# Stores, pair steps and first splits moved between engines in a fused attention, delta-rule and expert layer

## The chip, the cores and the metric

The kernel runs on one core of a Trainium2 chip. The core has a matrix engine (TensorE), a vector engine (VectorE), a scalar engine (ScalarE), GpSimd, and SyncE, which computes nothing. In this kernel SyncE, ScalarE and GpSimd issue transfers, each into its own queue in the trace, and the core's 16 DMA engines serve them all. The metric is the device time of one execution in microseconds, as the median of several runs.

## The reference

One layer in float32 on 512 tokens of width 1024. First come sliding-window attention with sinks (8 heads of 64, window 128) and a gated delta rule (4 heads of 128, chunks of 64) side by side, then the output weights `w_out` and a residual. The second half is an expert layer with product keys, and it takes most of the time:

```python
q = (xt @ w_q).reshape(T, 8, 2, 64)
s = einsum('thpc,hpnc->thpn', q, sub_keys)          # 128 keys in each half
s_top, i_top = top_k(s, 16)                         # then the 16 best of the 16 x 16 sums
gate = softmax(best_s)
act = gelu(einsum('tkd,td->tk', u_tab[idx], xn))    # 128 experts a token, out of 16384
out = h + einsum('tk,tkd->td', act * gate, v_tab[idx])
```

## The kernel before

Every matrix product is made of three, of a high and a low half of each operand in the reduced type: high by high, low by high, high by low. So each operand is split first: ScalarE copies the high half, and VectorE (or GpSimd) subtracts it from the original to get the low one. The program is a row of stages, each a block in which every engine has its own ordered list of instructions: `input_projection`, `prepare_mixers` (about 157 to 261 us), `recurrence` (to 321), `output_projection` (to 408), `routing` (to 857) and `experts` (to the end). PSUM banks are handed round by `Banks`, in the order in which their uses are added.

`prepare_mixers` makes for each of four blocks of 128 tokens the products of keys with keys (`kk`) and with queries (`qkT`), and from the first a chain of five levels that inverts a triangular matrix. `level_0` makes its first matrices (L1015) from which TensorE transposes `B0T` (L810), and `start` (L1021, L1023) makes the start of the inverse, which the levels (L749) work on. `keep_turning` (L167) issues matmuls of the identity between stages.

The expert layer is dense for tokens 128 to 511, and sparse for tokens 0 to 127. For the dense part there are 128 tiles of `u` and `v`, each 128 experts by 1024. An up product is 24 matmuls of 128x384 (L1980 to L1982 in routing, L2252 to L2254 in experts), followed by a gelu on ScalarE, and a down product is 18 matmuls of 128x512 (L2264 to L2266). Routing makes 80 up products (`EARLY`): 27 first, then one for each of 48 batches of 8 tokens, then 5 more. ScalarE stores their gelus in HBM from its own queue (L2039). Each batch also makes 16 small matmuls (L2007) of one-hot matrices, which VectorE and ScalarE prepare (L2098, L2046); ScalarE evicts them to `gate_stage` (L2062), and after every second batch SyncE stores 1 MB of gates in HBM (L1947), in the same ordered list as the loads of the u tiles (L1935, L1937), which go round 4 buffers (`NU`). Experts makes the other 48 up products, each beside a down product, and then 80 down products alone.

For tokens 0 to 127 GpSimd gathers single rows of a joint table (L1795), and VectorE takes 128 dot products (L1802) and 128 weighted sums (L1819), the pair steps, about 1.2 us each. `pair_steps` deals them out over the places, which are one batch of routing or one tile of experts. It adds a rate at each place and gives out steps while one is due, in groups of four dots and four adds; an add can't stand in the place of its own group's last dot.

```python
for rate in rates:
    due += rate
    here = []
    while at < len(todo) and due >= 1.0:
        what, k = todo[at]
        if what == "add" and k % GRP4 == 0 and ("dot", k + GRP4 - 1) in here:
            break
        here.append(todo[at])
        at, due = at + 1, due - 1.0
```

The rates give 145 steps to the first 48 places of experts, with one to six in a place, and in the last two of them one dot, and then four adds and a dot.

Of the kernel before, what the change touches and what calls it, by code (L numbers as in the profile page):

```python
# [6 lines left out]

# [5 lines left out]
P = 128  # L13
T = 512
TB = T // P
D = 1024
# [650 lines left out]
def prepare_mixers(nc, m, ps, sem, sinks, att_out_g, w_att_in, w_out):  # L667
# [16 lines left out]
    for b in range(TB):  # L684
        banks.add(("kk", b), "dve")
        banks.add(("qkT", b), "dve")
        if b:
            banks.add(("B0T", b - 1), "dve")
    banks.add(("B0T", TB - 1), "dve")
# [16 lines left out]
    with ExitStack() as ctx:  # L706
# [23 lines left out]
        with nc.Block() as block:  # L730
# [12 lines left out]
            def _(pe):  # L743
# [70 lines left out]
                for b in range(TB):  # L814
                    for g in ("kk", "qkT"):
                        banks.wait_free(pe, (g, b))
                        for h in range(DN):
                            rhs = m.unitT[:, (DN + h) if g == "kk" else h, b * P:(b + 1) * P]
                            t = nc.tensor.matmul(banks.bank((g, b))[:, h * P:(h + 1) * P],
                                                 m.unitT[:, DN + h, b * P:(b + 1) * P], rhs, start=True, stop=True)  # L820
                        t.then_inc(done, 1)
                    if b:
                        level_0_turn(b - 1)
                level_0_turn(TB - 1)
# [139 lines left out]
            def _(dve):  # L964
# [62 lines left out]
                for b in range(TB):  # L1027
# [12 lines left out]
                    if b:  # L1040
                        start(b - 1)
                start(TB - 1)
# [30 lines left out]
def recurrence(nc, m, ps, sem, wa_in, w_out_in, w_q_in, w_out, w_q, dn_out_g, x):  # L1073
# [20 lines left out]
    o_sq, o_ss, o_pow = sem("o_sq"), sem("o_ss"), sem("o_pow")  # L1094
# [3 lines left out]
    with ExitStack() as ctx:  # L1098
# [18 lines left out]
        with nc.Block() as block:  # L1117
# [68 lines left out]
            def _(dve):  # L1186
# [36 lines left out]
                for c in range(NC):  # L1223
# [51 lines left out]
            def _(act):  # L1275
# [8 lines left out]
                for c in range(NC):  # L1284
# [189 lines left out]
def output_projection(nc, m, ps, sem, w_out_in, w_q_in, early_u_in, u_t, norm_ffn_g, w_q, keys, h_dram, sel):  # L1474
# [33 lines left out]
    with ExitStack() as ctx:  # L1508
        sb = m.mem.local(ctx)
        gain = sb("ffn_gain", [P, D])  # L1510
        mixs = sb("mixT_split", [P, 2, KO, T], F32R)
        mixh, mixl = mixs[:, 0], mixs[:, 1]
        wh = sb("w_oq_h", [P, 4, KO, T], F32R)
# [7 lines left out]
        with nc.Block() as block:  # L1521
            @block.sync
            def _(sp):
                sp.dma_start(gain[:], norm_ffn_g[0:1, :].broadcast_to([P, D])).then_inc(g_in, 16)
                v = w_q[0].rearrange("(k p) n -> p k n", p=P)
                for i in range(2):

                    sp.wait_ge(w_lo, i + 1)
# [11 lines left out]
            def _(pe):  # L1540
# [15 lines left out]
                def hidden(g):  # L1556
                    half, b = g[1:]
                    pe.wait_ge(w_lo, half + 1)
# [4 lines left out]
                            lambda k: wh[:, half, k, :], lambda k: wl[:, half, k, :]).then_inc(done, 1)  # L1563

                def queries(g):
                    th, j = g[1:]
                    pe.wait_ge(w_lo, 4 if j < 2 else 6)
                    banks.wait_taken(pe, ("xT", 2 * th + 1, 1))
                    banks.wait_free(pe, g)
                    for e in range(2):  # L1570
                        h = 2 * j + e
                        v, c = slice((h % 4) * P, (h % 4 + 1) * P), slice(th * TH, (th + 1) * TH)
                        at = 2 if h < 4 else 0
# [41 lines left out]
            def _(act):  # L1615
                def split_w(i):
# [7 lines left out]
                    nc.scalar.activation(wh[:, i % 4], raw[i % 4], ACT.Copy).then_inc(w_hi, 1)  # L1624
# [28 lines left out]
                split_w(0)  # L1653
# [21 lines left out]
                for j in range(4):  # L1675
                    query_out(1, j)
                scores_out(2)
# [13 lines left out]
            def _(dve):  # L1691
                def split_w(i):
                    dve.wait_ge(w_hi, i + 1)
                    nc.vector.tensor_tensor(wl[:, i % 4], raw[i % 4], wh[:, i % 4].bitcast(F32),
# [35 lines left out]
                split_w(0)  # L1730
# [101 lines left out]
def pair_steps(rates):  # L1832
# [18 lines left out]
def routing(nc, m, ps, sem, u_in, next_u, u_t, v_rows, gates, gelus, pairs_of_0, steps, sel, nxt):  # L1851
# [6 lines left out]
    u_hi, u_lo = sem("early_u_hi"), sem("early_u_lo")  # L1858
# [45 lines left out]
    with ExitStack() as ctx:  # L1904
# [22 lines left out]
        with nc.Block() as block:  # L1927
            @block.sync
            def _(sp):
# [550 lines left out]
```

## Time and profile before

| | us |
|---|---|
| median of 3 runs | 1594.64 (1594.32 to 1595.9) |
| the profiled execution | 1595.65 |
| its span in the trace | 1593.9 |
| TensorE busy | 1527.5 (96%) |
| VectorE busy | 1322.2 (83%) |
| ScalarE busy | 715.8 (45%) |
| GpSimd busy | 349.2 (22%) |

The times of rows are microseconds from the span's start. A timeline's row is start, duration, engine, line, operation, output and inputs by their names, how many such instructions in a row, and in brackets how long the engine was idle before it and what released it. PE is TensorE, DVE VectorE, ACT ScalarE, POOL GpSimd, and SPq and ACTq are SyncE's and ScalarE's issues of transfers. Stretches of one engine overlap a little at their ends.

### The profile page before, as it was taken

Reading aid. Unit: us, or ns where it says so; the run is one execution under the profiler, and the core shown is the slowest. Engines: PE = TensorE matmul, PEld = TensorE weight load, DVE = VectorE, ACT = ScalarE, POOL = GpSimd, SP = SyncE. Lnnn points to the kernel's source line nnn. Section 1 sums busy time; section 2 is a strip of 40 time slices with the busy share of each in tenths; the row PEclk is TensorE's granted clock in tenths of the full one; section 3 lists DMA queues with packets and bytes.
Section 4 is the critical chain, followed back from the end, with each engine's and each line's share of the span. In section 5 each row is a group of like instructions: output and inputs, shape, how many; then the busy total and the mean of one; then the engine's idle time right before and its main releaser. Section 6 shows DMA issues by size and latency. Waiting matters only on the chain. (4 is left out here: it accounts for less than half of the span.)

```text
span 1593.9 us, 24872 instructions
## 1 busy us (share of the span) xinstructions
PE 1527.5 (96%) x9451; PEld 1389.4 (87%) x9451; DVE 1322.2 (83%) x2328; ACT 715.8 (45%) x1410; POOL 349.2 (22%) x301
## 2 busy tenths in 40 slices
PE   7999799999999999999998999999999999999999
PEld 6898688789999999999998999999999788888887
DVE  4638777776799999898874989998989889999996
ACT  4553453151343698788763333333333334333332
POOL 4011620110466100302230323232332211111100
PEclk9999899999999999999998999999999999999999
DMA  6220004030454477878997889898998899999972
GB/s 194 86 80 1 8 29 161 28 125 35 133 172 155 155 216 218 319 226 304 343 377 279 316 326 367 335 373 325 363 341 317 352 392 385 373 345 352 363 275 97
DMA packets 149931, 384.11 MB, mean 241 GB/s; under 512 B 10816, under 2 KB 91840, under 8 KB 131136
## 3 DMA queue, kind: packets, MB, share of 16 engines
q1 hardware_dynamic: 119872, 232.75, 41.8%
q0 software_dynamic: 18432, 134.23, 21.7%
q10 hardware_dynamic: 11520, 15.73, 2.7%
q8 instruction: 65, 1.06, 0.3%
q14 instruction: 42, 0.34, 0.1%
HBM read 337.58 MB, written 45.09 MB: 240 GB/s over the span
## 5 line engine op out<-in xcount | busy, mean ns | idle before, releaser
L1795 POOL DMA_INDIRECT scores<-in_peer_uv,pair_index x86 | 131.9, 1534 | 577.5 <-DVE pair_sum L1819 448.3
L1980 PE MATMUL bank<-x_hi,u_split 128*128 128x384 f32 x640 | 220.6, 345 | 16.4 <-DVE u_split L1917 10.8
L1982 PE MATMUL bank<-x_hi,u_split 128*128 128x384 f32 x640 | 215.9, 337 | 0.0
L1981 PE MATMUL bank<-x_lo,u_split 128*128 128x384 f32 x640 | 215.8, 337 | 0.0
L2264 PE MATMUL bank<-v_hi,act_hi 128*128 128x512 f32 x528 | 207.5, 393 | 3.4 <-DVE v_lo L2327 3.4
L2266 PE MATMUL bank<-v_hi,act_lo 128*128 128x512 f32 x528 | 206.9, 392 | 0.0
L2265 PE MATMUL bank<-v_lo,act_hi 128*128 128x512 f32 x528 | 206.7, 392 | 0.0
L2301 ACT ACTIVATE act_hi<-act_tile 128x384 fp32r<-128x384 f32 x128 | 66.9, 522 | 205.5 <-PE bank L2266 135.7
L2343 DVE TENSOR_TENSOR act_tile<-gelu_tile,onehots 128x384 f32<-128x384 f32 x128 | 117.9, 921 | 48.8 <-ACT gelu_tile L2312 37.3
L1980 PEld LDWEIGHTS bank<-x_hi,u_split 128*128 128x128 f32 x640 | 121.2, 189 | 18.7 <-ACT early_gelu L2036 10.3
L2252 PE MATMUL bank<-x_hi,u_split 128*128 128x384 f32 x384 | 129.1, 336 | 1.4 <-PEq L1927 1.4
L2254 PE MATMUL bank<-x_hi,u_split 128*128 128x384 f32 x384 | 129.0, 336 | 0.0
L2253 PE MATMUL bank<-x_lo,u_split 128*128 128x384 f32 x384 | 128.9, 336 | 0.0
L1981 PEld LDWEIGHTS bank<-x_lo,u_split 128*128 128x128 f32 x640 | 121.2, 189 | 0.0
L1982 PEld LDWEIGHTS bank<-x_hi,u_split 128*128 128x128 f32 x640 | 121.0, 189 | 0.0
L2046 ACT ACTIVATE onehot_gated<-onehot_i,rt_smallT 128x128 f32<-128x128 f32 x384 | 117.2, 395 | 7.2 <-DVE onehot_i L2098 6.8
L2264 PEld LDWEIGHTS bank<-v_hi,act_hi 128*128 128x128 f32 x528 | 99.8, 189 | 23.3 <-issue 3.8
L2266 PEld LDWEIGHTS bank<-v_hi,act_lo 128*128 128x128 f32 x528 | 99.7, 189 | 21.5
L2265 PEld LDWEIGHTS bank<-v_lo,act_hi 128*128 128x128 f32 x528 | 99.9, 189 | 19.6
L1795 POOL DMA_INDIRECT pair_rows<-in_peer_uv,pair_index x42 | 62.7, 1493 | 233.3 <-DVE pair_sum L1819 227.2
L1819 DVE SCALAR_TENSOR_TENSOR pair_sum<-scores,pair_c,pair_sum 128x1024 f32<-128x1024 f32 x86 | 107.4, 1282 | 0.7
L2327 DVE TENSOR_TENSOR v_lo<-v_raw,v_hi 128x1024 fp32r<-128x1024 f32 x88 | 107.2, 1219 | 0.4 <-ACT v_hi L2295 0.4
(325 smaller groups left out, 3654.9 us busy)
## 6 DMA issues: line engine op xcount, KB each, us to landing
v_raw<-in_peer_v SPq DMA_DIRECT2D x128, 512.0 KB, 7.2
u_raw<-in_peer_u SPq DMA_DIRECT2D x64, 512.0 KB, 6.2
u_raw_more<-in_peer_u SPq DMA_DIRECT2D x64, 512.0 KB, 6.9
gates<-gate_stage SPq DMA_DIRECT2D x24, 1024.0 KB, 5.8
onehots<-gates SPq DMA_DIRECT2D x16, 1536.0 KB, 10.8
early_gelus<-early_gelu ACTq DMA_DIRECT2D x80, 192.0 KB, 3.1
gelu_tile<-early_gelus SPq DMA_DIRECT2D x80, 192.0 KB, 7.1
w_raw<-in_w_in SPq DMA_DIRECT2D x9, 1024.0 KB, 5.2
```

The costliest lines, as they stand in the source:

```text
L1795: pool.indirect_dma_start(self.slot(k), None, self.table, bass.IndirectOffsetOnAxis(ap=self.sidx[:, k:k + 1], axis=0)).then_inc(self.lande ...
L1980: nc.tensor.matmul(banks.bank(g)[:, 0:TD], uh[:, q, w], m.xh[:, k, P:], start=(k == 0), stop=False)
L1981: nc.tensor.matmul(banks.bank(g)[:, 0:TD], uh[:, q, w], m.xl[:, k, P:], start=False, stop=False)
L1982: t = nc.tensor.matmul(banks.bank(g)[:, 0:TD], ul[:, q, w], m.xh[:, k, P:], start=False, stop=(k == KD - 1))
L2046: ins = nc.scalar.activation(og[:, slot(b, k), t, :], oi[:, slot(b, k), t, :], ACT.Copy, scale=smallT[:, b % 2, 1, k * BT + t:k * BT + t + 1])
L2252: nc.tensor.matmul(bank, uh[:, q, w], m.xh[:, k, P:], start=(k == 0), stop=False)
L2253: nc.tensor.matmul(bank, uh[:, q, w], m.xl[:, k, P:], start=False, stop=False)
L2254: t = nc.tensor.matmul(bank, ul[:, q, w], m.xh[:, k, P:], start=False, stop=(k == KD - 1))
L2264: nc.tensor.matmul(bank[:], ah[:, s, w], v_hi[:, c], start=first, stop=False)
L2265: nc.tensor.matmul(bank[:], ah[:, s, w], v_lo[:, c], start=False, stop=False)
L2266: t = nc.tensor.matmul(bank[:], al[:, s, w], v_hi[:, c], start=False, stop=last)
L2343: nc.vector.tensor_tensor(af[:], ge[n % NG2][:], gt[:, it % 2, :, jj], ALU.mult).then_inc(gate_f, 1)
```

## The change

Five edits. In `prepare_mixers` a list `opening` sets a new order of the banks of `kk`, `qkT` and `B0T` on TensorE, and VectorE's order follows it. The first half of `w_out` is split in the recurrence, into a buffer of its own (`w_first`), and the remaining weights take other places of `w_oq_h`. The first two u tiles are split at the end of `output_projection` (`u_split` now lies in the place of the first weights in `w_oq_h`) and not at the start of routing; GpSimd's low halves start with tile 2. The stores of the gates are issued by ScalarE, after the eviction of every second batch, and not by SyncE. `pair_steps` gives a place at most its rate rounded up, and the rates are 3.3 for 44 places and then 2.0 and 1.0, where they were 3.1 for 46. That gives 151 steps to the first 48 places of experts, at most four in one, and in the last two of them two adds and one add.

```diff
+    opening = [("kk", 0), ("qkT", 0), ("kk", 1), ("qkT", 1), ("B0T", 0), ("kk", 2), ("qkT", 2), ("kk", 3), ("B0T", 1),
+               ("B0T", 2), ("qkT", 3), ("B0T", 3)]
+    for g in opening:
+        banks.add(g, "dve")
...
-                for b in range(TB):
+                def gram(b):
                     dve.wait_ge(strict, 3 * b + 3)
                     banks.wait_full(dve, ("kk", b))
...
+                    banks.wait_taken(dve, ("kk", b))
+                    level_0(b)
+
+                def qk(b):
                     banks.wait_full(dve, ("qkT", b))
                     nc.vector.tensor_tensor(m.qkT[:, b], h4(banks.bank(("qkT", b))[:]), decT[:, b],
                                             ALU.mult).then_inc(banks.taken["dve"], 1)
-                    banks.wait_taken(dve, ("kk", b))
-                    level_0(b)
-                    if b:
-                        start(b - 1)
-                start(TB - 1)
+                gram(0)
+                qk(0)
+                gram(1)
+                qk(1)
+                start(0)
+                gram(2)
+                qk(2)
+                gram(3)
+                start(1)
+                start(2)
+                qk(3)
+                start(3)
...
+                    if c in (4, 6):
+                        dve.wait_ge(first_hi, 1)
+                        v = slice(c - 4, c - 2)
+                        nc.vector.tensor_tensor(m.w_first[:, 1, v, :], m.w_raw[0][:, KA + c - 4:KA + c - 2, :],
+                                                m.w_first[:, 0, v, :].bitcast(F32), ALU.subtract)
...
+                    if c == 3:
+                        act.wait_ge(w_out_in[0], 16)
+                        nc.scalar.activation(m.w_first[:, 0], m.w_raw[0][:, KA:], ACT.Copy).then_inc(first_hi, 1)
...
-
-                    sp.wait_ge(w_lo, i + 1)
+                    if i:
+                        sp.wait_ge(w_lo, 1)
                     sp.dma_start(raw[i], v[:, i * KO:(i + 1) * KO, T:]).then_inc(w_q_in[1], 16)
...
-                split_w(0)
                 for b in range(TB):
                     banks.wait_full(act, ("mixT", b))
...
                 for j in range(4):
                     query_out(1, j)
+                    if j == 2:
+                        for i in range(2):
+                            act.wait_ge(early_u_in[i], 16)
+                            banks.wait_full(act, ("q", 1, 1))
+                            nc.scalar.activation(uh[:, i, :], m.u_raw[i], ACT.Copy).then_inc(nxt.u_hi, 1)
...
+                for i in range(2):
+                    dve.wait_ge(nxt.u_hi, i + 1)
+                    nc.vector.tensor_tensor(ul[:, i, :], m.u_raw[i], uh[:, i, :].bitcast(F32),
+                                            ALU.subtract).then_inc(nxt.u_lo, 1)
                 scores_out(2)
                 scores_out(3)
...
-        while at < len(todo) and due >= 1.0:
+        while at < len(todo) and due >= 1.0 and len(here) < math.ceil(rate):
...
-                    if (k + 1) * BT % ST == 0:
-                        q = ((k + 1) * BT // ST - 1) % 2
-                        banks.wait_taken(sp, ("G", b, k, BT // 4 - 1))
-                        t0 = (b - 1) * P + (k + 1) * BT - ST
-                        sp.dma_start(gates[:, :, t0:t0 + ST, :].rearrange("g i t j -> i g (t j)"),
-                                     stage[:, q].rearrange("p g t j -> p g (t j)")).then_inc(stored[q], 16)
...
+                    if (k + 1) * BT % ST == 0:
+                        banks.wait_taken(act, ("G", b, k, BT // 4 - 1))
+                        t0 = (b - 1) * P + (k + 1) * BT - ST
+                        act.dma_start(gates[:, :, t0:t0 + ST, :].rearrange("g i t j -> i g (t j)"),
+                                      stage[:, half].rearrange("p g t j -> p g (t j)")).then_inc(stored[half], 16)
+
...
-                split_u(0)
-                split_u(1)
...
-                early_low(0)
...
-        rates = [2.0] * (P // 8) + [1.0, 2.0] + [3.1] * (NK - EARLY - 2) + [1.0] * EARLY
+        rates = [2.0] * (P // 8) + [1.0, 2.0] + [3.3] * (NK - EARLY - 4) + [2.0, 1.0] + [1.0] * EARLY
```

## Rows read from the trace of the kernel before

**Rows 1.** The page: busy time, share of the span, instructions of each engine.
```profile
PE 1527.5 (96%) x9451; PEld 1389.4 (87%) x9451; DVE 1322.2 (83%) x2328; ACT 715.8 (45%) x1410; POOL 349.2 (22%) x301
```

**Rows 2.** Waits of TensorE: us in all, times, the longest.
```profile
PE bank L1980 <- DVE u_split L1917: 10.8, 4, 8.5
PE bank L1980 <- POOL u_split L1917: 5.5, 4, 1.5
```

**Rows 3.** Windows: length, busy time of each engine, granted clock, DMA share, GB/s.
```profile
741.00:834.00 93.00, 91.29 (x604) 90.39 (x602) 78.20 (x82) 65.71 (x164) 28.80 (x16) 1.00 1.00 362
...
842.00:847.00 5.00, 4.78 (x15) 4.82 (x16) 1.30 (x2) 1.10 (x2) 0.00 (x0) 0.50 0.98 337
871.00:1238.00 367.00, 367.00 (x1867) 334.83 (x1865) 330.39 (x405) 129.24 (x196) 107.44 (x68) 1.00 0.88 339
1254.00:1260.00 6.00, 5.63 (x13) 4.46 (x14) 5.79 (x10) 2.06 (x3) 0.00 (x0) 0.50 1.02 424
```

**Rows 4.** Timelines of TensorE and VectorE in the preparation's opening.
```profile
179.86 1.09 PE L810 MATMUL bank<-ident,m_level 128*128 128x128 f32 x4 [4.57 <-DVE m_level L1015]
...
186.10 0.76 DVE L973 TENSOR_TENSOR att_sc<-bank,att_mask 128x256 f32<-128x256 f32 x2 [1.76 <-PE bank L764]
```

**Rows 5.** Timelines of ScalarE and TensorE at the output stage's start.
```profile
320.76 1.91 ACT L1624 ACTIVATE w_oq_h<-scores 128x2048 fp32r<-128x2048 f32 x1 [5.18 <-PEq L1117]
...
323.58 2.12 PE L167 MATMUL bank<-ident 128*128 128x128 f32 x12
```

**Rows 6.** Timelines of ScalarE, VectorE and TensorE around the routing stage's start.
```profile
402.28 0.60 ACT L1641 ACTIVATE qT<-bank 128x512 f32<-128x512 f32 x1 [5.16 <-PE bank L1553]
...
404.25 1.52 DVE L1726 COPY scores<-bank 128x512 f32<-128x512 f32 x2 [5.25 <-PE bank L1590]
...
410.49 0.44 PE L1980 MATMUL bank<-x_hi,u_split 128*128 128x384 f32 x1 [0.19 <-DVE u_split L1917]
```

**Rows 7.** SyncE in routing: its wait for the gates, and its longest issues.
```profile
SPq L1947 <- ACT gate_stage L2062: 161.7, 23, 11.9
...
653.49 14.57 SPq L1935 DMA_DIRECT2D u_raw_more<-in_peer_u  x1
...
753.75 8.63 SPq L1935 DMA_DIRECT2D u_raw_more<-in_peer_u  x1
...
778.17 9.56 SPq L1935 DMA_DIRECT2D u_raw_more<-in_peer_u  x1
...
805.89 9.21 SPq L1935 DMA_DIRECT2D u_raw_more<-in_peer_u  x1
...
828.53 12.29 SPq L1935 DMA_DIRECT2D u_raw_more<-in_peer_u  x1
```

**Rows 8.** Timelines of ScalarE and TensorE in routing.
```profile
658.41 0.33 ACTq L2039 DMA_DIRECT2D early_gelus<-early_gelu  x1
...
809.35 0.33 ACTq L2039 DMA_DIRECT2D early_gelus<-early_gelu  x1
...
839.75 1.06 ACT L2026 ACTIVATE u_split<-u_raw 128x1024 fp32r<-128x1024 f32 x1 [11.67 <-DMA u_raw<-in_peer_u]
...
842.22 0.66 PE L1980 MATMUL bank<-x_hi,u_split 128*128 128x384 f32 x1 [8.51 <-DVE u_split L1917]
```

**Rows 9.** Queues in 655 to 660: packets, MB, share of the 16 engines.
```profile
q0 software_dynamic: 247, 1.78, 86.2%
...
q1 hardware_dynamic: 149, 0.08, 5.0%
```

**Rows 10.** Timelines of VectorE and TensorE at the end of the experts' first part.
```profile
1243.34 0.92 DVE L2343 TENSOR_TENSOR act_tile<-gelu_tile,onehots 128x384 f32<-128x384 f32 x1 [4.25 <-ACT gelu_tile L2312]
...
1245.62 4.87 DVE L1819 SCALAR_TENSOR_TENSOR pair_sum<-scores,pair_c,pair_sum 128x1024 f32<-128x1024 f32 x4
...
1253.00 1.22 DVE L2327 TENSOR_TENSOR v_lo<-v_raw,v_hi 128x1024 fp32r<-128x1024 f32 x1
...
1254.37 0.77 PE L2264 MATMUL bank<-v_hi,act_hi 128*128 128x512 f32 x1 [3.42 <-DVE v_lo L2327]
```

More of the change, by code:

```diff
@@ L8 @@
+import math
 from contextlib import ExitStack
@@ L812, in level_0_turn, with gram @@
                     t.then_inc(done, 1)
[L814 to L824, printed above, removed]
+                def gram(g):
+                    banks.wait_free(pe, g)
+                    b = g[1]
+                    for h in range(DN):
+                        rhs = m.unitT[:, (DN + h) if g[0] == "kk" else h, b * P:(b + 1) * P]
+                        t = nc.tensor.matmul(banks.bank(g)[:, h * P:(h + 1) * P],
+                                             m.unitT[:, DN + h, b * P:(b + 1) * P], rhs, start=True, stop=True)
+                    t.then_inc(done, 1)
+                for g in opening:
+                    if g[0] == "B0T":
+                        level_0_turn(g[1])
+                    else:
+                        gram(g)
                 scores(0, 0)
@@ L1026, in _ @@
                 idb = m.ident[:].unsqueeze(1).broadcast_to([P, DN, P])
-                for b in range(TB):
+                def gram(b):
                     dve.wait_ge(strict, 3 * b + 3)
@@ L1509, in output_projection, with place @@
         sb = m.mem.local(ctx)
+        wh = m.mem.take("w_oq_h", [P, 4, KO, T], F32R, at_end=True)
+        m.u_split = m.mem.over("u_split", [P, 4, D], "w_oq_h", F32R)
+        uh, ul = m.u_split[:, 0:2], m.u_split[:, 2:4]
+        def place(i):
+            return (i + 2) % 4
         gain = sb("ffn_gain", [P, D])
@@ L1557, in hidden @@
                     half, b = g[1:]
-                    pe.wait_ge(w_lo, half + 1)
+                    w = [m.w_first[:, 0], m.w_first[:, 1]]
+                    if half:
+                        pe.wait_ge(w_lo, 1)
+                        w = [wh[:, place(1)], wl[:, place(1)]]
                     banks.wait_taken(pe, ("mixT", b))
@@ L1562, in hidden @@
                     product(banks.bank(g)[:], range(KO), lambda k: mixh[:, k, v], lambda k: mixl[:, k, v],
-                            lambda k: wh[:, half, k, :], lambda k: wl[:, half, k, :]).then_inc(done, 1)
+                            lambda k: w[0][:, k, :], lambda k: w[1][:, k, :]).then_inc(done, 1)
                 def queries(g):
                     th, j = g[1:]
-                    pe.wait_ge(w_lo, 4 if j < 2 else 6)
+                    pe.wait_ge(w_lo, 3 if j < 2 else 5)
                     banks.wait_taken(pe, ("xT", 2 * th + 1, 1))
@@ L1623, in split_w @@
                         banks.wait_full(act, ("h", 1, TB - 1))
-                    nc.scalar.activation(wh[:, i % 4], raw[i % 4], ACT.Copy).then_inc(w_hi, 1)
+                    nc.scalar.activation(wh[:, place(i)], raw[i % 4], ACT.Copy).then_inc(w_hi, 1)
                 def square(b):
@@ L1692, in split_w @@
                 def split_w(i):
-                    dve.wait_ge(w_hi, i + 1)
-                    nc.vector.tensor_tensor(wl[:, i % 4], raw[i % 4], wh[:, i % 4].bitcast(F32),
+                    dve.wait_ge(w_hi, i)
+                    nc.vector.tensor_tensor(wl[:, place(i)], raw[i % 4], wh[:, place(i)].bitcast(F32),
                                             ALU.subtract).then_inc(w_lo, 1)
@@ L1960, in _ @@
             def _(pool):
-                for n in range(1, FIRST):
+                for n in range(2, FIRST):
                     pool.wait_ge(u_hi, n + 1)
-                    if n == 1:
-                        pool.wait_ge(u_lo, 1)
                     u_low(nc.gpsimd, n).then_inc(u_lo, 1)
@@ L2164, in experts @@
         uh, ul = m.u_split[:, 0:2, :], m.u_split[:, 2:4, :]
-        h = m.mem.over("h_rows", [P, TB, D], "u_split")
+        h = m.mem.over("h_rows", [P, TB, D], "w_oq_h_kept")
+        ah = sb("act_hi", [P, NA, TD], F32R)
+        al = sb("act_lo", [P, NA, TD], F32R)
         vh2 = sb("v_hi", [P, 2, D], F32R)
@@ L2419, in hybrid_layer @@
         w_out_in, w_q_in = [[sem(f"{name}{i}") for i in range(2)] for name in ("w_out_in", "w_q_in")]
+        m.w_first = mem.take("w_first", [P, 2, D // P // 2, T], F32R, at_end=True)
         m.acc = mem.take("acc", [P, TB, D])
         recurrence(nc, m, ps, sem, w_att_in, w_out_in, w_q_in, a["w_out"], a["peer_w_q"], a["dn_out_norm_g"], a["x"])
-        mem.drop("z", "wqT", "u", "qkT", "kdec", "egrow")
+        mem.drop("z", "wqT", "u", "qkT", "kdec", "egrow", "w_first")
         m.xh = mem.take("x_hi", [P, KD, T], F32R, at_end=True)
@@ L2427, in hybrid_layer @@
         early_u_in, u_in = [[sem(f"{name}{i}") for i in range(NU)] for name in ("early_u_in", "u_in")]
+        nxt = Tensors()
+        nxt.u_hi, nxt.u_lo = sem("early_u_hi"), sem("early_u_lo")
         sgate, sidx = mem.take("pair_gate", [P, HA]), mem.take("pair_index", [P, HA], U32)
@@ L2439, in hybrid_layer @@
         pairs_of_0 = Gathered(nc, sem, slots, m.mix[:, 0, :], sidx[:], sgate[:], a["peer_uv"], mem.take)
-        rates = [2.0] * (P // 8) + [1.0, 2.0] + [3.1] * (NK - EARLY - 2) + [1.0] * EARLY
+        rates = [2.0] * (P // 8) + [1.0, 2.0] + [3.3] * (NK - EARLY - 4) + [2.0, 1.0] + [1.0] * EARLY
         steps = pair_steps(rates)
         before, after = steps[:P // 8], steps[P // 8:]
-        m.u_split = mem.take("u_split", [P, 2 * 2, D], F32R)
         m.early_gelu = mem.take("early_gelu", [P, 2, TD])
```

23 lines of the change are left out of this document (7 added, 16 removed).

## The prediction, before the change was run

> **What bounds the kernel now.** I read the page first: TensorE is busy 96% of the span of 1593.9 us, so all that a change of order can give lies in about 66 us of its idle time and in stretches of half clock [rows 1]. The chain of waits of TensorE then says where that idle time is. Two of its lines are in the routing stage, both ahead of the up products (L1980): 10.8 us in 4 waits for VectorE's low half of a u tile, of which one is 8.5 us long, and 5.5 us in 4 waits for GpSimd's low half [rows 2]. The windows show what kind of time the rest is. In 741 to 834 the 16 DMA engines are busy all the time, at 362 GB/s, with VectorE busy 78.20 us of 93; in 842 to 847, right after the 8.5-us wait, the granted clock is 0.50 (1.2 GHz of 2.4) [rows 3]. In the experts' first part VectorE is busy 330.39 of 367 us while TensorE is never idle, and in 1254 to 1260 the clock is 0.50 once more [rows 3]. Last come the timelines around each place that the diff touches [rows 4 to 10].
>
> **The preparation's opening.** The change lets TensorE and VectorE take the key products of blocks 2 and 3 earlier, and VectorE does the query product of block 3 and the start of its inverse last. What moves is order; no instruction is added. TensorE waits 4.57 us for the last level matrix [rows 4]. That wait mostly goes, but what TensorE does next still needs the last start of the inverse (L1021, L1023), and that stays the last thing in VectorE's line before the attention scores. Later is VectorE's own 1.76-us wait for attention scores of TensorE [rows 4]: those come out earlier now, by what is taken from TensorE's late work. Of this 1.76 I take a half, **-0.8 us**. The bounds are 0 (VectorE finishes the same work at the same time) and -1.8 (the whole of the wait).
>
> **The first w_out half, split in the recurrence.** Removed from the output stage: ScalarE's copy of 1.91 us at 320.76 and VectorE's subtraction. Added to the recurrence: the same copy, in ScalarE's waits in the recurrence, of which the last is the 5.18 us ahead of this very copy [rows 5], and two subtractions of 128x1024 at 1.22 [rows 10], in VectorE's waits before the chunk's fill matmuls end. TensorE gains little: between the transposes and the first product it turns 12 idle matmuls for 2.12 us to 325.70, and these stay [rows 5]; the first product can't come before them. I take **-0.2**. If the two subtractions are on the recurrence's chain, it is +2.4; if the turning matmuls were started earlier by the freed engines, -0.8.
>
> **The first two u tiles, split in the output stage.** ScalarE's two copies (1.06 each, as the one in [rows 8]) go into a wait of 5.16 us, VectorE's two subtractions (1.22 each) into one of 5.25 us [rows 6], so both are hidden; without that cover they would cost up to 2.1 and 2.4. At the routing's start TensorE waits 0.19 us behind its turning matmuls for the first low half [rows 6]: **-0.2**. VectorE and ScalarE start the stage some 2 to 2.6 us ahead. GpSimd keeps its 25 low halves, which take longer when VectorE is busy beside it; the 5.5 us of waits [rows 2] may move by 3 us either way, and I take 0.
>
> **The pair steps, capped.** At the end of the experts' first part VectorE does four adds (4.87 us from 1245.62) and a dot (1.22) before the gate product and the low half of the v tile, which starts at 1253.00; TensorE waits 3.42 us for that and starts at 1254.37 [rows 10]. Then the clock is 0.50 for about 6 us, 1254 to 1260, with 13 matmuls [rows 3]: half the speed loses half the time, 2.9. After the change this place has one step, not five; the one before has two, not one, but VectorE waits 4.25 us for a gelu between them [rows 10], which takes that up. So four steps fewer stand ahead of the low half, 4 x 1.22 = 4.9 us: it would end at 1249.3, and TensorE gets free at 1254.37 - 3.42 = 1250.95. **-6.3** for wait and clock together. What pays for it: 151 steps, not 145, in 48 places. In the window of 367 us there are 1867 matmuls, 42 a place, so 44.4 places of 8.26 us, with VectorE busy 7.44 in each [rows 3]; 0.2 steps more at 1.22 make 7.7. It fits on average; a place of four dots and its 3.9 of other work is 8.8, and places of five and six steps are gone. Bounds: 0 (a wait at another place takes the gain) and -6.3.
>
> **The gates' stores on ScalarE's queue.** SyncE spends 161.7 us in 23 waits for gate_stage, in order ahead of the u loads [rows 7]. Behind a gate store the next load's issue is held: 14.57, 8.63, 9.56, 9.21 and 12.29 us for the five longest [rows 7]. The loads then come late: ScalarE waits 11.67 us for a u tile up to 839.75, and TensorE 8.51 up to 842.22 [rows 8]. The gate store is 1 MB in pieces of 512 bytes, and the u loads share its queue. In 655 to 660 that queue moves 149 packets and 0.08 MB while the gathers' queue moves 247 packets and 1.78 MB [rows 9]: the queues take turns by packet and not by byte, so loads behind small packets wait longest. *Removed:* all late-load waits (10.8 less the 0.19 at the start, 10.6) and the half clock after them, 5 us [rows 3], so 2.5: 13.1 us. *Moved:* 24 issues of about 0.4 us each to ScalarE, 9.6 us, which has 65.71 of 93 us busy [rows 3]; and with them the blocking. Behind a gate store ScalarE's next issue is a gelu store, 4.92 us after SyncE's blocked issue in one place and 3.46 in the other [rows 7, 8]. It is now 0.33 us even while SyncE is held from 653.49 on [rows 7, 8], so the blocking belongs to the queue, and it moves too. The holds left are 14.57 - 4.92 = 9.7, 9.21 - 3.46 = 5.8, and with 4.2 for the others 4.4, 5.4 and 8.1. What ScalarE has in hand: a place is 93/604 x 40 = 6.2 us, ScalarE is 29% idle, 1.8 a place, and its copy of a u tile can come two places less an up product (4.2, the 24 long matmuls of a place's 40) and both halves' splits (2.3) ahead, 5.9. So a hold is hidden up to 3.6 (two places' idle time, if VectorE, 84% busy, hands on every delay) and up to 1.8 + 5.9 = 7.7. I take 5.0, nearer to the low end since VectorE can't make up: what is left is 4.7 + 0.8 + 0.4 + 3.1 = 9.0. **13.1 - 9.0 = -4.1 us.** The bounds are -13.1 (nothing is blocked, all loads in time) and, with the holds on the path in full and a half clock after the two long ones, 33.4 + 5 - 13.1 = +25.
>
> The Trainium skill speaks against this step: its page "DMA: Bandwidth & Descriptors", section "Issuing engines are not separate DMA queues", says that DMAs started by another engine run on the same 16 DMA engines and save only the sequencer's time of issue. By that the step gives 0 in place of -4.1. The same page, section "Queues, rings and completion order", has each DMA engine take turns between queue rows by packet, and with that the row of 655 to 660 agrees (more packets of the gathers, but far more bytes); by it the loads do gain.
>
> **Sum.** -0.8 - 0.2 - 0.2 - 6.3 - 4.1 = -11.6: a span of 1582.3. The profiled execution took 1595.65, 1.75 more than its span, and is 1.0 above the median of 1594.64. So 1582.3 + 1.75 - 1.0 = **1583.0 us** as the median.
>
> **Rivals.**
> *The stores pay in full* (-13.1): -0.8 - 0.2 - 0.2 - 6.3 - 13.1 = -20.6, 1574.0. For it: a load that has a queue of its own gets a turn for each packet, and its packets are large. Against: the holds on ScalarE are as long as on SyncE if the blocking is by queue, and the gelu stores follow within 5 us.
> *A new queue gives nothing* (0): the 16 engines are at 1.00 in 741 to 834 [rows 3], so bytes that come earlier for one come later for another, and the 8.51 us return. The sum is -7.5, 1587.1. Against it is the 0.08 MB of [rows 9]. This is what the page's rule on issuing engines would make of it.
> *The capped steps only shift the wait.* VectorE, at 7.7 of 8.26 a place, waits for a gelu or for gathered rows, and the 3.42 us and the clock come back: with at most 0.5 us in hand a place, one late gather of 3 us is enough. Then -11.6 + 6.3 = -5.3, 1589.3.
> *The other side: ScalarE behind its own stores.* One mechanism: the gelu store's issue stands behind 1 MB of 512-byte packets, and evictions and one-hot scaling stand behind it on ScalarE, so TensorE waits at its banks. Its price is up to 33.4 us of holds over the five, with the half clock +25 for the step, so 1594.6 - 7.5 + 25 = 1612. From 20.6 us of stalls in the routing's second half on (13.1 + 7.5) the kernel is slower than before; a middle case is 1600. For it: heavy stretches are just where the DMA engines are full. Against: the ScalarE issue rows of now, all 0.33.
>
> **Chances.** Forecast 0.38, own range 1579 to 1587; stores in full 0.24; new queue gives nothing 0.12; capped steps shift the wait 0.10; ScalarE blocked, at or past the turning point 0.16, of which 0.11 beyond 1597.8 and 0.05 between. 0.2% of the time, 3.2 us, is about what a measurement can tell from no change: faster is below 1591.4. Faster: 0.38 + 0.24 + 0.12 + 0.10 less 0.05 for tails = 0.79; same 0.10; slower 0.11. The range leaves out the blocked case and the far end of the full one: 1572.5 to 1592.
>
> **What would show it.** Right: no wait before L1980's counterpart near 840 and no clock of 0.50 there; ScalarE's waits for u_raw gone; issues of early_gelus of several us after a gate store on ScalarE's queue, none on SyncE; no 3.4-us wait at about 1240 before the v tile's first matmul; the 4.57-us wait of the opening gone but the first level's sums only about 0.8 earlier; the first product of the output and routing stages right at the end of the turning matmuls. Wrong: gelu issues that stay at 0.33 (then the stores pay in full); u tiles as late as before (nothing); waits of L2007 for ScalarE's one-hots after each store (the other side); waits at v_lo at 1100 to 1240 (the steps).

## The result and the profile after

The changed kernel takes 1602.31 us as the median of 10 runs (1597.88 to 1607.08), the kernel before 1592.56 (1587.55 to 1595.9, 10 runs, the three shown above among them). The ratio is 1.0064, with a 95% interval of 1.0052 to 1.0075: slower by 0.64%, some 10 us. The forecast was 1583.0, with a range of 1572.5 to 1592.0; the time lies outside it, and on the other side.

The profiled execution took 1603.36 us, its span is 1601.6. TensorE's share is as before [rows 1]:

```profile
PE 1532.5 (96%) x9451; PEld 1392.7 (87%) x9451; DVE 1318.2 (82%) x2330; ACT 715.5 (45%) x1410; POOL 366.4 (23%) x300
```

TensorE's waits from routing to the start of the second part of experts (us in all, times, the longest), which answer to [rows 2]:

```profile
PE bank L2038 <- ACT onehot_gated L2077: 9.3, 3, 6.0
PE bank L2011 <- DVE u_split L1956: 7.0, 2, 6.9
PE bank L2011 <- POOL u_split L1956: 5.3, 4, 1.5
PE bank L2038 <- DVE onehot_j L2132: 5.1, 6, 1.6
PE bank L2011 <- ACT gate_stage L2093: 3.5, 3, 1.2
...
PE bank L2297 <- DVE v_lo L2360: 0.5, 1, 0.5
```

L2011 is the up product (L1980 before) and L2038 the product of one-hots (L2007). The first and fifth lines are new: TensorE waits for ScalarE's scaled one-hots and for its evictions. The 8.51-us wait for the low half of a u tile is down to 6.9, but not gone. The timelines say what ScalarE was doing, first at the worst place:

```profile
650.32 0.38 ACTq L2099 DMA_DIRECT2D gates<-gate_stage  x1
...
655.16 0.47 ACT L2067 ACTIVATE early_gelu<-bank 128x384 f32<-128x384 f32 x1
655.66 13.40 ACTq L2070 DMA_DIRECT2D early_gelus<-early_gelu  x1
669.16 1.08 ACT L2093 ACTIVATE gate_stage<-bank 128x512 f32<-128x512 f32 x2 [13.53 <-issue]
670.13 2.43 ACT L2077 ACTIVATE onehot_gated<-onehot_i,rt_smallT 128x128 f32<-128x128 f32 x8
```

The gate store itself is issued in 0.38 us. The next issue of the same queue, the gelu's store, takes 13.40 us, and ScalarE's evictions, one-hots and u tile stand behind it. There are six such holds: 13.40 us here, then 2.20 at 738.79, 7.36 at 762.69, 6.51 at 791.76, 6.07 at 819.97 and 7.12 at 847.86, 42.7 us together. They follow the six gate stores that are slow to land, 12.0 to 23.3 us after their issue (this one takes 23.3). The other 18 stores land in 5.1 to 8.7 us, and no issue of over 1.5 us follows them. SyncE's longest issue in routing is 2.20 us now. ScalarE no longer waits for a u tile's transfer. The last hold has a wait ahead of it that I hadn't named:

```profile
841.12 0.41 ACTq L2099 DMA_DIRECT2D gates<-gate_stage  x1
...
847.34 0.49 ACT L2067 ACTIVATE early_gelu<-bank 128x384 f32<-128x384 f32 x1 [3.80 <-DMA early_gelus<-early_gelu]
847.86 7.12 ACTq L2070 DMA_DIRECT2D early_gelus<-early_gelu  x1
855.10 1.06 ACT L2057 ACTIVATE u_split<-u_raw_more 128x1024 fp32r<-128x1024 f32 x1 [7.27 <-issue]
```

There are two gelu buffers, so a gelu waits for the store of the one before last, and that store now also lies in the queue with a gate store. Here there are up products alone, so TensorE is out of work soon. Its two longest waits stand behind the first hold and the last one:

```profile
671.55 3.75 PE L2038 MATMUL bank<-onehot_j,onehot_gated 128*128 128x128 f32 x16 [6.04 <-ACT onehot_gated L2077]
...
857.57 0.66 PE L2011 MATMUL bank<-x_hi,u_split 128*128 128x384 f32 x1 [6.88 <-DVE u_split L1956]
```

The windows (length, busy time of each engine, clock, DMA share, GB/s) show the price. After each of the two waits the granted clock is 0.50 (672 to 676, 858 to 861):

```profile
655.00:672.00 17.00, 10.91 (x67) 10.30 (x66) 10.99 (x29) 3.47 (x11) 0.00 (x0) 0.94 1.01 399
672.00:676.00 4.00, 4.00 (x19) 4.00 (x19) 2.45 (x3) 3.16 (x7) 0.00 (x0) 0.50 0.31 81
741.00:834.00 93.00, 85.45 (x559) 83.08 (x558) 76.36 (x83) 64.81 (x166) 35.34 (x13) 1.00 0.90 317
849.00:862.00 13.00, 6.12 (x26) 5.83 (x25) 2.45 (x2) 2.98 (x4) 0.00 (x0) 0.74 0.96 337
858.00:861.00 3.00, 3.00 (x11) 3.00 (x11) 1.22 (x1) 0.57 (x2) 0.00 (x0) 0.50 0.79 215
871.00:1238.00 367.00, 366.47 (x1860) 334.14 (x1859) 334.99 (x411) 128.67 (x197) 117.46 (x69) 1.00 0.90 345
1262.00:1272.00 10.00, 10.00 (x45) 8.19 (x45) 9.79 (x13) 4.43 (x6) 1.01 (x1) 1.00 1.01 416
```

In 741 to 834 TensorE runs 559 matmuls where it ran 604 [rows 3], and the DMA engines are less busy than before, 0.90 at 317 GB/s: bandwidth isn't what it waits for. The end of the experts' first part went as the prediction said, no wait and no half clock (the last line, against [rows 10] and the window of 1254 to 1260 in [rows 3]). And 871 to 1238 holds something that no part of the prediction speaks of: TensorE is idle for half a microsecond only, yet runs 1860 matmuls where it ran 1867.

Both kernels run 9451 matmuls, nearly all in the same order, so that the start of the n-th can be compared (each number is a difference of two starts in a trace):

| matmuls | what | before | after |
|---|---|---|---|
| 860 to 1240 | preparation's opening | 47.28 | 45.49 |
| 2500 to 3320 | output stage, routing's start | 113.72 | 112.98 |
| 3320 to 4680 | first up tiles, first batches | 226.72 | 226.69 |
| 4680 to 6080 | rest of routing | 233.05 | 247.61 |
| 6080 to 7960 | experts, first part | 369.13 | 372.27 |
| 7960 to 8040 | its end | 24.58 | 18.31 |
| 8040 to 9450 | experts, second part | 322.43 | 322.74 |

The rest of routing costs 14.6 us more, the end of the experts' first part gives 6.3, the opening 1.8 and the output stage with routing's start 0.7, and 3.1 are lost in the experts' first part. The traces differ by another 1.5 us in matmuls 0 to 860 (142.04 and 140.53), which no edit touches.

### The profile page after: what moved, and what is told of

The parts are those of the page before. It is cut to its first block and busy times, and to the rows that moved or that the text cites. A ratio compares the mean times of both kernels' runs of the same rounds, so it can differ in the third digit from the quotient of the medians.

```text
span 1601.6 us, 24872 instructions
## 1 busy us (share of the span) xinstructions
PE 1532.5 (96%) x9451; PEld 1392.7 (87%) x9451; DVE 1318.2 (82%) x2330; ACT 715.5 (45%) x1410; POOL 366.4 (23%) x300
## 5 line engine op out<-in xcount | busy, mean ns | idle before, releaser
L1834 POOL DMA_INDIRECT scores<-in_peer_uv,pair_index x86 | 141.7, 1648 | 570.3 <-DVE pair_sum L1858 439.8
L2011 PE MATMUL bank<-x_hi,u_split 128*128 128x384 f32 x640 | 220.1, 344 | 15.9 <-DVE u_split L1956 7.0
L2011 PEld LDWEIGHTS bank<-x_hi,u_split 128*128 128x128 f32 x640 | 121.1, 189 | 18.4 <-ACT early_gelu L2067 7.2
L1834 POOL DMA_INDIRECT pair_rows<-in_peer_uv,pair_index x42 | 71.1, 1692 | 211.7 <-DVE pair_sum L1858 204.9
L2038 PE MATMUL bank<-onehot_j,onehot_gated 128*128 128x128 f32 x768 | 97.1, 280 | 14.6 <-ACT onehot_gated L2077 9.3
```

What stands on the lines that cost most here:

```text
L1834: pool.indirect_dma_start(self.slot(k), None, self.table, bass.IndirectOffsetOnAxis(ap=self.sidx[:, k:k + 1], axis=0)).then_inc(self.lande ...
L2011: nc.tensor.matmul(banks.bank(g)[:, 0:TD], uh[:, q, w], m.xh[:, k, P:], start=(k == 0), stop=False)
```

## The experiments

Theory Q: the hold goes with the queue, moved to ScalarE with the stores, and its length on ScalarE's path is the loss. Rival S: the new steps and their order load VectorE too much. Rival B: the DMA engines are full and it makes no difference whose queue it is.

**One edit undone, and two edits alone.** e1 is the changed kernel with this edit taken back, e2 the kernel before with it:

```diff
-                        sp.dma_start(gates[:, :, t0:t0 + ST, :].rearrange("g i t j -> i g (t j)"),
+                        act.dma_start(gates[:, :, t0:t0 + ST, :].rearrange("g i t j -> i g (t j)"),
```

e3 is the kernel before with only the cap and the new rates of `pair_steps`.

> The changed kernel with one edit undone: the gates' stores are issued by SyncE again. Theory Q (the queue holds the next issue behind a 1-MB store in 512-byte pieces, and on ScalarE that hold is the loss): in the two traces TensorE's lag grows from -2.8 us at 641 to +10.5 at 861, so undoing it gives 13 us back: 1589 us where the changed kernel has 1602.3, a little faster than before (1592.6), with the gelu issues at 0.33 us and the 8.5-us wait near 840 in place again. Rival S (the loss is VectorE with 3.3 steps a place and the dearer order, not the queue): 1600 or more. Rival B (the DMA engines are full, so it makes no difference whose queue it is): 1600 or more as well, with late u tiles.

> The kernel before with the gates' stores alone moved to ScalarE. Theory Q: the whole loss and more, 13 us slower than before, about 1605.5, with holds of 6 to 14 us on the gelu store that follows. Rival S: no slower than before, 1590 to 1593. My forecast's own size for this edit was -4.1: 1588.5.

> The kernel before with the cap and the new rates alone. Theory Q with what the two traces show of this part (6.3 us less at the end of the first part, but 3.2 us of new waits spread over 900 to 1250): -3, 1589.5. My forecast was -6.3: 1586.3. Rival S: slower than before, 1600.

Measured: e1 1587.25 us, 0.9974 of the kernel before (0.9961 to 0.9986); e2 1606.27, 1.0091 (1.0074 to 1.0109); e3 1589.0, 0.9976 (0.9964 to 0.9988). The median of before in these runs was 1591.03. Theory Q gave 1589, 1605.5 and 1589.5. Rivals S and B fall: the stores alone cost 15 us wherever they are added or taken out, and the steps are a gain. Over matmuls 4680 to 6080 the traces give the stores 20.1 us against e1 (247.61 and 227.5) and 13.6 in e2 (246.69 and 233.05). In e1 TensorE's wait near 840 is back at 832.23, but with 3.96 us and not the 8.5 that was expected. In e2 the holds are 12.73, 3.25, 7.09, 6.50 and 5.94 us, so they don't hang on the other edits. In e3 the end of the first part takes 18.2 us as in the changed kernel, but a wait has come at another place:

```profile
997.28 1.23 DVE L1803 SCALAR_TENSOR_TENSOR scores<-scores,mix 128x1024 f32<-128x1024 f32 x1 [2.52 <-DMA scores<-in_peer_uv,pair_index]
...
1001.26 1.22 DVE L2328 TENSOR_TENSOR v_lo<-v_raw,v_hi 128x1024 fp32r<-128x1024 f32 x1
...
1002.62 0.70 PE L2265 MATMUL bank<-v_hi,act_hi 128*128 128x512 f32 x1 [3.10 <-DVE v_lo L2328]
```

VectorE waited for a gathered row, with 1.27 us for another just ahead, and the low half of a v tile came 3.1 us late: the prediction's rival of the shifted wait, once, and it took 5.0 of the 6.3 us in this trace. In the changed kernel the same place costs 0.9.

**The gelus' stores off that queue.** e4 is the changed kernel with the gelus' stores on SyncE, each behind the load of the u tile five ahead, so that on ScalarE's queue only the next gate store stands behind a gate store, two places later:

```diff
+                def store_gelu(n):
+                    banks.wait_taken(sp, ("up", n))
+                    sp.dma_start(gelus[n], ge[:, n % 2, :]).then_inc(nxt.ge_out[n % 2], 16)
...
                     load_u(early(n) + NU)
+                    store_gelu(early(n) - 1)
...
-                    banks.wait_taken(act, ("up", n))
-                    act.dma_start(gelus[n], ge[:, n % 2, :]).then_inc(nxt.ge_out[n % 2], 16)
```

> The changed kernel, gates' stores still on ScalarE, but the stores of the gelus now on SyncE behind the loads, so that the next issue behind a gate store on ScalarE's queue comes two places later. Theory Q: no hold reaches ScalarE's computing; all late-load waits are gone too, and the time is 1580 (1602.3 less some 22 us of waits that the five holds led to). If the queue is still not drained after two places where the DMA engines are full (holds of up to 2 us at the next gate store), 1585. Rival B: bytes and packets are the same, so the waits come back elsewhere: 1597 or more.

Measured: 1582.46 us, 0.9943 (0.9927 to 0.996), 20 us less than the changed kernel and 8.6 less than before. One hold is left, of a gate store behind a gate store, and TensorE loses nothing to it. ScalarE's timeline, and the windows around it and later:

```profile
647.23 0.37 ACTq L2106 DMA_DIRECT2D gates<-gate_stage  x1
...
660.51 7.02 ACTq L2106 DMA_DIRECT2D gates<-gate_stage  x1
667.56 1.28 ACT L1391 ACT_TABLE_LOAD   x1 [7.08 <-issue]
```

```profile
649.00:667.00 18.00, 17.26 (x114) 16.31 (x113) 17.83 (x43) 9.47 (x24) 3.21 (x2) 1.00 1.00 400
741.00:834.00 93.00, 93.00 (x615) 93.00 (x614) 77.90 (x82) 66.35 (x161) 26.43 (x15) 1.00 1.05 388
```

TensorE is never idle in 741 to 834, at 388 GB/s where it was 362 before [rows 3] and 317 with the change. So 362 GB/s was no ceiling.

**What a hold is for.** e7 changes the layout of the gates in HBM, and nothing about who stores what: a store is 128 rows of 8 KB, and the experts' gate loads read the 512-byte pieces.

```diff
-    gates = nc.dram_tensor("gates", [NK // GJ, NK, TD, GJ], F32, kind="Internal").ap()
+    gates = nc.dram_tensor("gates", [TD // 16, NK, NK // GJ, 16 * GJ], F32, kind="Internal").ap()
...
-                        act.dma_start(gates[:, :, t0:t0 + ST, :].rearrange("g i t j -> i g (t j)"),
+                        act.dma_start(gates[t0 // ST],
```

> The changed kernel with gates and gelus stored by ScalarE as in it, but the gates laid out in HBM so that a store is 128 rows of 8 KB instead of 2048 pieces of 512 bytes; the experts' 16 gate loads then read 512-byte pieces in its stead. Theory P (the hold behind a store is for its number of packets): the gelu issues behind a store are at 0.33 us, routing is as short as with the gelus on SyncE, 20 us less than in the changed kernel up to the stage's end, and the holds appear behind the gate loads on SyncE in the experts stage, where they cost nothing or a few us: 1582 to 1590. Rival (the hold is for the bytes of the store, 1 MB): holds of 6 to 13 us as before, 1602.

Measured: 1587.59 us, 0.9966 (0.9951 to 0.9982), 15 us less than the changed kernel. There is no hold at all on ScalarE's queue; the issues behind that same place:

```profile
651.43 0.33 ACTq L2099 DMA_DIRECT2D gates<-gate_stage  x1
657.67 0.33 ACTq L2070 DMA_DIRECT2D early_gelus<-early_gelu  x1
```

ScalarE's queue in 600 to 860 (packets, MB, share of the 16 engines), first in the changed kernel, then in e7, and the landing of e7's store of 651.43:

```profile
q10 hardware_dynamic: 44832, 27.59, 34.3%
```

```profile
q10 hardware_dynamic: 8784, 28.18, 27.5%
...
gates<-gate_stage ACTq DMA_DIRECT2D x1, 1024.0 KB, 13.3
```

About the same bytes in a fifth of the packets, and that store is still under way when the gelu's store behind it is issued in 0.33 us, 6.2 us after it and 7 before its landing. So the hold goes with a store of many small packets and not with a megabyte under way. Whether the number of packets or their size counts, e7 doesn't tell apart. Matmuls 4680 to 6080 take 219.8 us, the least of all kernels.

The holds come back where the expectation put them, on SyncE behind the experts' gate loads, which read 512-byte pieces now. From 1230 on there are nine of 6.5 to 13.5 us, where the changed kernel has none over 1.3. One of them, and TensorE's waits from 1249.9 to 1590 (us in all, times, the longest; none in the changed kernel):

```profile
1267.91 0.43 SPq L2233 DMA_DIRECT2D onehots<-gates  x1
1270.26 13.50 SPq L2244 DMA_DIRECT2D gelu_tile<-early_gelus  x1
...
PE bank L2297 <- DVE v_lo L2360: 6.3, 8, 2.3
```

Matmuls 8040 to 9450 take 332.3 us (322.7 in the changed kernel). That is 9.6 us, more than the few that were expected; 6.3 are these waits for low halves of v tiles, and what the rest is no run shows.

**The slower pace of the experts' first part.** Leaving out matmuls 6700 to 6780, where VectorE's late row can fall, the matmuls 6080 to 7960 take 353.5 us in the kernel before, e2 and e3 and 355.8 in the changed kernel, e1 and e4: it goes with the layout of the tiles, not with who issues what. Down matmuls start 0.2274 us apart in the one group and 0.2289 in the other (the median of the 44 down products), and the up matmuls are slower too, 0.1734 and 0.1745. e5 is e4 with the tiles at the memory's end on multiples of 128 bytes; e6 is the kernel before with the v tiles 64 bytes further on; the act tiles laid behind them moved by 128 bytes with it, which the expectation doesn't say.

```diff
-        at = gaps[-1][1] if at_end else gaps[0][0]
+        at = gaps[-1][1] // 128 * 128 if at_end else gaps[0][0]
```

> The version with gelu stores on SyncE, and every tile that is laid at the end of the memory moved down to a multiple of 128 bytes (a loss of 64 bytes). It tests a second difference of the traces: in the experts' first part a down product's matmuls start 0.2290 us apart in the changed kernel and 0.2270 before, 3.1 us over 1880 matmuls, in every run with the changed layout and in none with the old one, whoever issues what. In the changed layout v_hi and v_lo begin 64 bytes off a multiple of 128, before they were on one. Theory L (that offset): 0.2270 again, 3 us less, 1579.5 where that version had 1582.5. Rival: another property of the layout (which tiles lie side by side, the distance of act and v tiles), or the pair steps: 0.2290 and 1582.5.

> The kernel before with v_hi and v_lo alone shifted by 64 bytes. Theory L: down matmuls 0.2290 apart instead of 0.2270, in the second part (v tiles at the same shift) too where these tiles are used. Rival: 0.2270. The time by itself can't tell; the trace does.

e5: 1581.27 us, 0.9937 (0.9919 to 0.9955), the pace still 0.2289. e6: 0.2328 in the first part and 0.2333 in the second, where it was 0.2287, and 1602.19 in its one run. Theory L falls as the cause of the change's slower pace. The shifts of e6 do cost time, and more than the change's. Its trace says something of which tile does it. In the second part every other down product reads `v_hi_late` and `v_lo_late`, which e6 leaves where they are, and these slow down as well: 0.2298 us a matmul before, 0.2333 in e6. So there the 64 bytes of the v tiles aren't needed, and what such a product reads from another address is the act tiles. (`gelu_tile3`, which TensorE doesn't read, moves with them.) Two kernels for the order of the tiles followed: e9 is e5 with `act_hi` and `act_lo` taken behind the v tiles, e10 the kernel before with them taken ahead.

> The kernel of e5 with the halves of the activations laid after the v tiles (v_hi at 99712, v_lo at 130944, act_hi at 107904, act_lo at 139136) and not before them. The offset of 64 bytes has fallen as a cause, since all these tiles lay on 128 in e5 and the pace stayed at 0.2289 us. Theory N (the pace goes with the order or the neighbours of the act and v tiles): another pace, 0.2267 to 0.2274, and 3 us less than the 1581.3 of e5. Rival (it goes with u_split's or h_rows' new place, which this leaves): 0.2289 and 1581.3.

> The kernel before with the activations' halves laid before the v tiles, as the change does, and nothing else: act_hi 116096, act_lo 122240, v_hi 128384, v_lo 136576. Theory N: 0.2289 us between the down products' matmuls in the first part in place of 0.2274. Rival: 0.2274.

e9: 1584.96 us, 0.9945 (0.9929 to 0.9961), pace 0.2289. e10: pace 0.2274 (one run, 1592.91). Theory N falls. What is left of the layout is `u_split` and `h_rows`. e12 is e4 with the third part of the change undone (`u_split` taken where it was, the first two u tiles split at routing's start, `h_rows` over it).

```diff
-        m.u_split = m.mem.over("u_split", [P, 4, D], "w_oq_h", F32R)
...
+        m.u_split = mem.take("u_split", [P, 2 * 2, D], F32R)
```

> The version with gelu stores on SyncE (e4), with the third part undone: the first two u tiles are split at routing's start again, u_split lies at 72064 and h_rows over it, and so all tiles of the expert layer have the addresses of the kernel before. The order of act and v tiles has fallen as a cause of the slower pace (e9, e10). Theory U (the pace goes with u_split's place): 0.2274 us between down matmuls and 0.1734 between up matmuls in the experts' first part, 3.2 us less, and 0.7 more for the splits that return to routing's start: 2.5 less than e4's 1582.5, 1580. Rival (it goes with the new rates of the pair steps, that is with VectorE's work): the steps are kept here, so 0.2289 and 1583.2. The run with the steps alone (e3) at 0.2274 speaks against that already.

e12: 1580.84 us, 0.9920 (0.9904 to 0.9935), and the pace is 0.2274 again: 353.5 us for the same matmuls. So the slower pace comes with the third part of the change. Moving the act and v tiles by themselves doesn't give it (e10); `u_split`, `h_rows` and all that shifts with them (the one-hots' tiles by 16 KB) weren't told apart, and why a matmul's pace should depend on it, no run shows.

**The steps, and the queues alone.** e8 is e5 with the old pair steps; e11 is the kernel before with the gates' stores on ScalarE and the gelus' on SyncE.

> The first kernel of this call with the old pair steps (no cap, 3.1). In the traces the end of the experts' first part (40 matmuls around the change to down products alone) takes 24.6 us with the old steps and 18.3 with the new ones, and nothing is lost ahead of it once the layout is set aside. So 6 us slower than the first kernel of this call, 1585.5. If the capped steps cost as much before (3.3 in place of 3.1 steps a place, a late gather), as the run with the steps alone suggests (2.0 us gained): 2 us slower, 1581.5.

> The kernel before with both queue moves and nothing else: gates' stores on ScalarE, gelus' stores on SyncE. If the parts of the change simply add: e4 stood 9 us below before and e1 (all of the change but the gates' stores) 4 us below, so the queues alone are worth 5 to 6 us, 1586.5. If the traces' stage times hold instead (routing after the first up tiles 222.0 in e4, 233.0 before): 11 us, 1581. If the gain in e4 hung on the other edits (the earlier u tiles above all): no faster than 1591.

e8: 1585.9 us, 0.996 (0.9947 to 0.9974), 4.6 more than e5. Its 3.4-us wait at the end of the first part is back:

```profile
1245.98 0.47 PE L2304 MATMUL bank<-v_hi,act_hi 128*128 128x512 f32 x1 [3.40 <-DVE v_lo L2367]
```

e11: 1587.56 us, 0.9964 (0.9949 to 0.998). Matmuls 4680 to 6080 take 223.4 us, 9.7 less than in the profiled run of before, but the median stands only 5.3 below: the parts add up as medians, and the one trace of before has the longest late load of the kernels with the gates on SyncE (233.05; 230.48, 230.64 and 232.6 in e3, e6 and e10; 227.5 in e1).

## Why the prediction was wrong

**The step that failed** is "I take 5.0, nearer to the low end since VectorE can't make up: what is left is 4.7 + 0.8 + 0.4 + 3.1 = 9.0". The mechanism is the one that the prediction names: the hold moves with the stores to the gelu's store. What was mis-sized is what it leaves on the path: 247.61 - 222.01 = 25.6 us over matmuls 4680 to 6080, the changed kernel against e4, and not 9.0. Three things made the term:

- The holds are 42.7 us over six places and not 33.4 over five, with 13.40 for my 9.7. I let the queue be free 15.0 us after the gate store's issue, as on SyncE (653.07 to 668.06), and it was 18.7 (650.32 to 669.06).
- ScalarE had much less in hand than 5 us for each. I had reckoned its lead over the u tiles alone, but evictions and one-hots stand behind the hold as well, and the waits for them are most of the new ones (9.3 and 3.5 us, against 7.0 for u tiles). The late store of the gelu before last came on top, 3.8 us just where there are up products alone. In this stretch TensorE waits 24.7 us in the changed kernel and 5.4 in e4, 19.3 more.
- The 9.0 have nothing for the clock (the prediction counts it in its upper bound alone), which is 0.50 after the two longest waits and never in e4. The 6.3 us that are left of the 25.6 go with it.

So 25.6 us of stalls came of 42.7 us of holds, 60%. The step's other half, the late loads at 13.1 us, was too large, but by less: e4, where they are gone, takes 11.0 us less than before, and 5.5 to 10.6 less than e1, e3, e6 and e10, the other kernels with the gates on SyncE. The prediction put the turning point, from which the kernel is slower, at 20.6 us of stalls, 13.1 + 7.5. With what the traces show it is 11.0 + 6.3 + 1.8 + 0.7 - 3.1 = 16.7, and 25.6 lies beyond either. It gave the case 0.16 and ended the range short of it.

**A queue of its own** does bring the loads in time: ScalarE's 11.67-us wait is gone, and e4 shows what it is worth once nothing stands behind the stores. The rival that a new queue gives nothing, and the rule of the Trainium skill behind it ("DMA: Bandwidth & Descriptors", "Issuing engines are not separate DMA queues"), give 0 for e11; it measured 5.3 us. The rule's other sentence, that initiating elsewhere saves only the sequencer's time, "which is usually small relative to the DMA itself", is where this case departs: the sequencer's time was 13.40 us for one issue.

**The capped steps** gave the 6.3 us at their place, in every trace (24.6 to 18.3, or 23.5 to 18.2). As medians they are worth 4.6 (e8 against e5) and 2.0 (e3), since a late gathered row near matmul 6700 takes back 0.6 to 5 us, a rival that the prediction had as all or nothing. Its place of four dots is a little dear: 7.44 less 3.1 steps at 1.22 leaves 3.7 us of other work and not 3.9, so 8.5 and not 8.8, still above 8.26.

**The opening** gave 1.2 us, forecast 0.8: 45.5 us on average over the eight traces with it (44.9 to 45.8) and 46.8 over the six without (46.1 to 47.3). TensorE's 4.57-us wait is 0.7 us now, and the first level's sums (L1049) start 0.9 us earlier against matmul 860: 190.27 - 149.94 = 40.33 before, 187.94 - 148.49 = 39.45 after. But not by the step that I took: VectorE's 1.76-us wait [rows 4] is 1.79 after. In these two traces it is the small copy behind it (L979) that got shorter, from 1.15 us to 0.17. That isn't the step for all kernels: four others with the old opening have a wait of 1.0 us there and a copy of 0.7, less together than the changed kernel. So the size is near the forecast by luck, and by which step the opening gains stays open.

**The first w_out half** gave 0.3 us, forecast 0.2. From the output stage's first transpose to its first product it is 4.96 us before (320.79 to 325.75) and 4.67 after (317.57 to 322.24), and e2, e3 on one side and e1, e4 on the other repeat the two numbers within 0.03. **The first u tiles** gave 0.4 us, forecast 0.2: from the first of the 18 turning matmuls to the first up product it is 2.35 us before (408.14 to 410.49) and 1.92 after (404.63 to 406.55), and 2.35 again in e12, which undoes this part. They cost 2.3 by the pace of the experts' first part, for which the prediction has no term: it put a change of address at nothing, without a reason.

## What to carry to other kernels

Before moving a store to another engine's queue, look for the next issue on that queue and for what the engine computes behind it: a store of 2048 small pieces is issued in 0.4 us, and where it is slow to land, the issue behind it pays, up to 13.4 us. Such a store wants a queue whose next issue is far off (e4), or larger pieces (e7). When buffers get new addresses, compare the spacing of matmuls in a stretch without waits before any wait is explained.

## What the hardware showed that I had not expected

The address of tiles changes TensorE's pace without any wait: 0.2274, 0.2289 and 0.2328 us between the same matmuls of 128x512 at full clock, in three layouts. The last one, with v tiles 64 and act tiles 128 bytes further on, costs 2% of that pace, also in products that read the v tiles which stayed. Windows of 900 to 1200, before (a part of the one in [rows 3]) and in e6, both without idle time:

```profile
900.00:1200.00 300.00, 300.00 (x1531) 274.25 (x1530) 268.14 (x328) 104.05 (x158) 89.76 (x56) 1.00 0.91 349
```

```profile
900.00:1200.00 300.00, 300.00 (x1510) 270.38 (x1508) 265.32 (x324) 104.05 (x158) 81.58 (x56) 1.00 0.90 346
```

Some of the spread of one kernel's runs, up to 9 us here, can come from a place that the change hardly touches. In the recurrence the same matmuls (2000 to 2390) take 38.7 to 44.0 us over the traces, the longer the lower the clock granted in 262 to 284: 38.7 in e4 and 44.0 in e12, whose windows follow, and 40.7 before, with a clock of 0.84. Each kernel has one trace, so that the runs of one kernel differ by this is argued and not shown.

```profile
262.00:284.00 22.00, 18.80 (x116) 15.27 (x114) 15.99 (x35) 5.52 (x6) 1.21 (x2) 1.00 0.78 284
```

```profile
262.00:284.00 22.00, 19.17 (x85) 15.35 (x85) 13.16 (x29) 5.77 (x6) 0.00 (x0) 0.69 0.79 289
```
